# Expert weights for gate and up read in rows of 16 KB instead of 4 KB, in a one-core trunk step

## The chip, the core and the metric

The kernel runs on one core of a Trainium2 chip. The metric is the device time of one execution in microseconds (us): the median of three executions was 2595.72 us, the lowest 2595.25, the highest 2600.82.

## What is computed

One layer of a diffusion trunk with hybrid mixers, in fp32, for 512 latent tokens and 128 context tokens of 2048 channels: adaLN modulation, one input projection into attention heads and S5 groups, one output projection, and then a routed feed-forward network with 16 experts. Every expert picks its 64 best latent tokens and its 16 best context tokens. The change lies wholly in that last part:

```python
def expert_choice_ffn(x, p):
    B, L, D = x.shape
    cap = CAPACITY_FACTOR * L // N_EXPERTS
    aff = jax.nn.softmax((x @ p['w_router']).astype(jnp.float32), axis=-1)
    g, idx = lax.top_k(jnp.swapaxes(aff, 1, 2), cap)
    bidx = jnp.arange(B)[:, None, None]
    xs = x[bidx, idx]
    h = (jax.nn.silu(jnp.einsum('becd,edf->becf', xs, p['w_gate']))
         * jnp.einsum('becd,edf->becf', xs, p['w_up']))
    y = jnp.einsum('becf,efd->becd', h, p['w_down']) * g[..., None].astype(x.dtype)
    return jnp.zeros_like(x).at[bidx, idx].add(y)
```

w_gate and w_up are 16 x 2048 x 1024, w_down is 16 x 1024 x 2048, all fp32: 8 MB each per expert, 24 MB an expert, 384 MB in all. Every matrix is read once.

## The kernel before

It is written engine by engine, with semaphores set by hand. Up to about 1490 us it does the modulation, the projections, attention and S5, the output projection and the routing. Then the experts run one after the other on PE (TensorE), from fully unrolled code, while SP issues all weight transfers, POOL the gathers and scatters of tokens, and ACT and DVE evict and multiply.

**Pieces and the ring.** The weights of an expert come in 12 pieces of 2 MB. Pieces 0 to 7 are gate (even) and up (odd): piece j has 4 blocks of 128 channels, 4 * (j // 2) to 4 * (j // 2) + 3, each with all 1024 columns. Seen from a partition that is four rows of 1024 floats (4 KB), 512 KB apart in the matrix, since `w_gate_v` (L413) puts channel `k * 128 + p` into block k and partition p. Pieces 8 to 11 are down: two blocks of 128 hidden units each, rows of 2048 floats (8 KB). `piece` (L578) issues one piece into one of eight slots of the ring `w_ring` (L262). Two of the slots were in use earlier by other buffers, so that the first eight pieces (gate and up of expert 0) are issued one by one as space comes free.

**The order.** `ORDER` (L417) interleaves gate and up of expert e with down of expert e - 1, as PE uses them: two gate/up pieces, one down piece. `next_piece` (L606) waits until PE has used up the piece that lay in the slot eight pieces earlier (`s_used`), and then issues the next one; SP does nothing else in this stage.

**PE.** `expert` (L1438) goes through nine steps j. In step j it does `gate_up(j)` for expert e (for j < 8), `down(j - 1)` for expert e - 1 (for j > 0), and after steps 2, 4, 6 and 8 it turns four blocks of the tokens of expert e + 1 (`turn_four`, L1396). `gate_up` (L1410) waits for its piece, then uses each 64 columns of it as the stationary operand and the 80 turned tokens as the moving one, accumulating over all 2048 channels in PSUM. Each fp32 product shows as two MATMUL records and two LDWEIGHTS records, so that a piece makes 128 of each at L1419. `down` (L1424) has the tokens stationary and 512 columns moving (L1433). The first gate_up of an expert has to wait for ACT and DVE to take the hidden activations of the expert before out of PSUM (`s_hh`).

**Tokens.** `gather` on POOL (L1961) fetches the 80 rows of 8 KB of the expert's tokens into `xs`, one token to a partition. `turn_four` turns 80 x 128 columns at a time into PSUM bank 7 (through the helper at L985, where all turnings of the kernel have their records), and ACT (L962) copies four of them at a time to `xsT`, whose block k is the moving operand for block k of gate and up. `scatter` (L1971) adds the results to the rows of the output.

Of the kernel before, what the change touches and what calls it, by code (L numbers as in the profile page):

```python
# [13 lines left out]
P = 128  # L14
# [19 lines left out]
SLOTS = CAP_L + CAP_C  # L34
# [11 lines left out]
BIAS_OFF = [16, 8, 0]  # L46
START = 12
RING_SLOTS = 8


class Chain:
# [28 lines left out]
def trunk_step(nc, t, out):  # L80

    ctx = ExitStack()
    with ctx:
# [27 lines left out]
        def bank(b, n=BANK, at=0):  # L111
            return PS[:, b * BANK + at:b * BANK + at + n]
# [148 lines left out]
        RING = RING_SLOTS  # L261
        w_ring = [work[:, i * 4096:(i + 1) * 4096] for i in range(1, RING - 1)] + [hT_[:, 6144:6144 + 4096], work[:, 0:4096]]  # L262
        gate2 = mixT_[0:SLOTS, 0:D]
        xs = [mixT_[0:SLOTS, D * (1 + i):D * (2 + i)] for i in range(2)]
# [125 lines left out]
        s_w = [sem(f"s_w{i}") for i in range(RING)]  # L390
# [19 lines left out]
        w_in_v = t["w_in"].rearrange("(k p) n -> p k n", p=P)  # L410
        w_ada_v = t["w_ada"].rearrange("(k p) n -> p k n", p=P)
        w_out_v = t["w_out"].rearrange("(k p) n -> p k n", p=P)
        w_gate_v = t["w_gate"].rearrange("e (k p) n -> p e k n", p=P)  # L413
        w_up_v = t["w_up"].rearrange("e (k p) n -> p e k n", p=P)
        w_down_v = t["w_down"].rearrange("e (k p) n -> p e k n", p=P)

        ORDER = [0, 1, 8, 2, 3, 9, 4, 5, 10, 6, 7, 11]  # L417
# [28 lines left out]
        def _(sp):  # L446
# [5 lines left out]
            with sp.Fori(0, ADA_MIX // 2) as i:  # L452
                for s in range(2):
                    n = 2 * i + s
# [64 lines left out]
            for qc in range(16):  # L519
                src = bass.AP(t["rpb"].tensor, qc, [[RPB_W, 8], [RPB_W * RPB_H, HEADS], [1, SPAN]])  # L520
# [33 lines left out]
            for n in range(4):  # L554
                s = n % 2
# [22 lines left out]
            def piece(e, j, r):  # L578

                dst = w_ring[r % RING]  # L580
                if j < 8:
                    src = (w_gate_v, w_up_v)[j % 2][:, bass.ds(e, 1), 4 * (j // 2):4 * (j // 2) + 4, :]
                    dst = dst.rearrange("p (k n) -> p k n", k=4)
                else:
                    src = w_down_v[:, bass.ds(e, 1), 2 * (j - 8):2 * (j - 8) + 2, :]
                    dst = dst.rearrange("p (k n) -> p k n", k=2)
                sp.dma_start(dst, src.rearrange("p e k n -> p (e k) n")).then_inc(s_w[r % RING], 16)  # L587

            sp.wait_ge(s_omm, START + 15)
            piece(0, 0, 0)  # L590
# [26 lines left out]
            last = 24 * (EXPERTS // 2 - 1)  # L617
# [365 lines left out]
        def _(pe):  # L983
            def turn(dst, src, parts=P):
                return pe.transpose(dst, src, ident[0:parts, 0:parts])  # L985
# [398 lines left out]
            for tt in range(4):  # L1384
                pe.wait_ge(s_aff, tt + 1)
                last = turn(bank(0, P, P * tt)[0:EXPERTS, :], aff[:, tt, :])
# [9 lines left out]
            def turn_four(e, s, b):  # L1396

                pe.wait_ge(s_xsev, 4 * e + b)
                for k in range(4 * b, 4 * b + 4):
                    last = turn(bank(7, SLOTS, (k - 4 * b) * SLOTS), xs[s][:, k * P:(k + 1) * P], SLOTS)  # L1400
                last.then_inc(s_xsT, 1)

            def hidden_at(u, f):
# [644 lines left out]
```

## Time and profile before

| | |
|---|---|
| median of three runs | 2595.72 us |
| the profiled execution, its own time | 2594.34 us |
| its span, from the first instruction to the last | 2592.6 us |
| PE busy / PEld (weight loads, beside PE) | 2328.6 us (90%) / 1542.8 us (60%) |
| DVE, ACT, POOL busy | 583.8, 341.4, 291.2 us |
| bytes moved by DMA | 628.81 MB in 243174 packets |
| gate and up products (L1419), the slots in `work`, 14336 MATMUL | 540.6 us, 237 ns each |
| down products (L1433), 2688 MATMUL with tokens from `hT_` and weights from `work` | 310.8 us, 595 ns each |
| chain that ended last: SP's piece issues (L587) | 18% |

Matmuls overlap, so a mean of 237 ns is the length of one record and not its cost: the 128 records of one gate_up take 4.65 us together. PEld is the loading of the stationary operand, which runs beside PE. The granted clock (PEclk) is a share of full speed: 1.00 is 2.4 GHz, 0.50 is 1.2 GHz. "issue" is idle time of an engine in which it waited for nothing that the profile shows. A packet is one contiguous piece of a transfer that one of the 16 DMA engines moves; the share of a queue is the time that its packets took, of the time of all 16 engines in the window, and can come to a little over 100% because packets overlap.

### The profile page before, as it was taken

To read this page: it belongs to the slowest core of one execution; us is meant where nothing else is said; L and a number is where in the kernel's file an instruction comes from. 1 tells how busy PE (TensorE), PEld (TensorE's weight loads), DVE (VectorE), ACT (ScalarE), POOL (GpSimd) and SP (SyncE) were. 2 spreads that over 40 slices of the span, in tenths; PEclk is the share of its full clock that TensorE was granted. 3 is DMA by queue.
4 is the path that set the end of the run, shared out by engine and by line. 5 is a ranking of instruction groups with operands and counts; after the bars stand their busy time and mean duration, and the time that the engine had idled before them with its cause. 6 is when DMAs were issued, how large, how long until landed. Compare 5 with 4: busy or idle time off the path is not lost.

```text
span 2592.6 us, 57318 instructions
## 1 busy us (share of the span) xinstructions
PE 2328.6 (90%) x26381; PEld 1542.8 (60%) x26381; DVE 583.8 (23%) x882; ACT 341.4 (13%) x726; POOL 291.2 (11%) x375
## 2 busy tenths in 40 slices
PE   2599999999999999999999469999999998889997
PEld 1177888745555565554445366666666666666663
DVE  2242332034444433331103500000000000000001
ACT  2121111112322232321003100000000000000000
POOL 3060665000000000000021100000000000000000
PEclk8799999999999999999999689999999999999999
DMA  8921221585565621324222599999999999999996
GB/s 284 361 71 54 78 59 54 97 294 195 174 222 184 217 67 36 111 92 146 77 112 102 201 357 358 390 395 395 395 389 393 382 392 383 389 385 390 401 398 221
DMA packets 243174, 628.81 MB, mean 243 GB/s; under 512 B 14106, under 2 KB 96020, under 8 KB 220724
## 3 DMA queue, kind: packets, MB, share of 16 engines
q1 hardware_dynamic: 219904, 578.29, 59.6%
q0 software_dynamic: 3072, 20.97, 3.5%
q10 hardware_dynamic: 19972, 26.02, 3.1%
q8 instruction: 205, 3.36, 0.5%
q14 instruction: 21, 0.17, 0.0%
HBM read 600.77 MB, written 24.48 MB: 241 GB/s over the span
## 4 chain that ended last, share of the span: by engine, by line
PE 62%; SPq 18%; DMA 5%; DVE 4%; issue 3%; ACT 2%; ACTq 1%; POOL 0%; DVEq 0%; POOLq 0%
SPq L587 18%; PE PS L1239 14%; PE PS L1419 11%; PE PS L1330 11%; PE PS L1057 10%; PE PS L1433 6%; PE PS L985 2%; DMA work<-in_w_gate 2%; DVE work L1691 2%; PE PS L1267 2%; DMA work<-in_w_up 1%; PE PS L1227 1%; PE PS L1370 1%; PE PS L1252 1%; PE PS L1094 1%
## 5 line engine op out<-in xcount | busy, mean ns | idle before, releaser
L1419 PE MATMUL PS<-hT_,work 128*64 128x80 f32 x14336 | 540.6, 237 | 69.8 <-issue 54.9
L1419 PEld LDWEIGHTS PS<-hT_,work 128*64 128x64 f32 x14336 | 521.2, 140 | 115.0 <-issue 86.5
L1239 PE MATMUL PS<-hT_,work 128*128 128x512 f32 (+1 forms) x1536 | 439.4, 436 | 0.0
L1239 PEld LDWEIGHTS PS<-hT_,work 128*128 128x128 f32 x1536 | 223.8, 191 | 156.8 <-issue 156.8
L1433 PE MATMUL PS<-work,hT_ 128*32 128x512 f32 (+1 forms) x2688 | 310.8, 595 | 4.2 <-DVE mixT_ L1821 2.7
L1057 PE MATMUL PS<-work,hT_ 128*128 128x256 f32 x1280 | 284.5, 383 | 1.2 <-DVE hT_ L1555 1.2
L1330 PE MATMUL PS<-work,mixT_ 128*128 128x512 f32 x640 | 279.6, 597 | 0.0
L1057 PEld LDWEIGHTS PS<-work,hT_ 128*128 128x128 f32 x1280 | 243.5, 192 | 35.2 <-issue 2.1
L1807 DVE TENSOR_TENSOR hT_<-PS,hT_ 128x480 f32<-128x480 f32 x16 | 10.5, 657 | 982.3 <-ACT hT_ L968 982.3
L1330 PEld LDWEIGHTS PS<-work,mixT_ 128*128 128x128 f32 x640 | 121.7, 192 | 149.0 <-issue 149.0
L1433 PEld LDWEIGHTS PS<-work,hT_ 128*32 128x32 f32 (+1 forms) x2688 | 76.1, 105 | 163.8 <-issue 151.1
L962 ACT ACTIVATE hT_<-PS 128x320 f32<-128x320 f32 x64 | 28.0, 437 | 924.9 <-PE PS L985 924.9
L1691 DVE RECIPROCAL work<-work 128x640 f32<-128x640 f32 x24 | 99.7, 4153 | 158.9 <-ACT work L880 158.9
L1981 POOL DMA_INDIRECT out_y<-mixT_,work x16 | 23.0, 1440 | 861.6 <-DVE mixT_ L1821 861.6
L985 PE MATMUL PS<-consts,work 128*128 128x128 f32 (+3 forms) x441 | 68.2, 280 | 42.8 <-DVE work L1758 15.5
L985 PEld LDWEIGHTS PS<-consts,mixT_ 80*128 80x128 f32 (+3 forms) x403 | 39.8, 154 | 106.3 <-issue 65.5
L985 PE MATMUL PS<-consts,mixT_ 80*128 80x80 f32 (+3 forms) x403 | 52.1, 270 | 53.1 <-DVE mixT_ L1529 26.7
L1940 POOL TENSOR_TENSOR work<-work,consts 128x256 f32<-128x256 f32 x36 | 26.3, 760 | 623.6 <-DVE small L1677 548.0
L985 PEld LDWEIGHTS PS<-consts,work 128*128 128x128 f32 (+3 forms) x441 | 52.3, 151 | 52.0 <-DVE work L1758 16.0
L1009 PE MATMUL PS<-work,cT 128*2 128x512 f32 x256 | 40.2, 789 | 47.6 <-DMA work<-in_b_ada 47.6
L1419 PEld LDWEIGHTS PS<-hT_ 128*64 128x64 f32 x2048 | 72.0, 137 | 13.2 <-DMA hT_<-in_w_gate 8.6
L1419 PE MATMUL PS<-hT_ 128*64 128x80 f32 x2048 | 74.8, 233 | 5.4 <-DMA hT_<-in_w_gate 4.1
(241 smaller groups left out, 1656.4 us busy)
## 6 DMA issues: line engine op xcount, KB each, us to landing
work<-in_w_up SPq DMA_DIRECT2D x57, 2048.0 KB, 26.4
work<-in_w_down SPq DMA_DIRECT2D x56, 2048.0 KB, 26.7
work<-in_w_gate SPq DMA_DIRECT2D x55, 2048.0 KB, 23.9
work<-in_w_ada SPq DMA_DIRECT2D x32, 2048.0 KB, 9.4
work<-in_w_in SPq DMA_DIRECT2D x80, 512.0 KB, 4.8
work<-in_w_ada SPq DMA_DIRECT2D x8, 4096.0 KB
hT_<-in_w_gate SPq DMA_DIRECT2D x9, 2048.0 KB, 30.5
work<-in_w_out SPq DMA_DIRECT2D x4, 4096.0 KB, 13.7
```

Of the source, the lines that this page charges most:

```text
L587: sp.dma_start(dst, src.rearrange("p e k n -> p (e k) n")).then_inc(s_w[r % RING], 16)
L962: act.activation(xsT[s][:, 4 * b:4 * b + 4, :].rearrange("p k s -> p (k s)"), bank(7, 4 * SLOTS), ACT.Copy).then_inc(s_xsev, 1)
L985: return pe.transpose(dst, src, ident[0:parts, 0:parts])
L1009: last = pe.matmul(bank(2 + s)[q:q + 2, :], cTv[:, :, k], w_ada_ring[s][:, k, :], start=(k < 4), stop=(k >= KT - 4))
L1057: last = pe.matmul(bank(n % 2, 256), hT[:, k, tt * P:(tt + 1) * P], w_chunk[chunk % NW][:, 256 * (k % 4):256 * (k % 4) + 256], start=(k == ...
L1239: last = pe.matmul(bank(2 * which, n, col), w_chunk[chunk % NW][:, HD * (k % 8):HD * (k % 8) + HD], hT[:, k, col:col + n], start=(k == 0), ...
L1267: last = pe.matmul(bank(4)[q:q + 2, :], cTv[:, :, 8 * x + k], late_ring[x][:, k, :], start=(x == 0 and k < 4), stop=(x == 1 and k >= 4))
L1330: last = pe.matmul(bank(tt), mix_at(k)[:, tt * P:(tt + 1) * P], w_out_ring[n % 2][:, k, :], start=(k == 0), stop=(k == HEADS - 1 if n == 0 ...
L1419: last = pe.matmul(hidden_at(u, f)[64 * h:64 * h + 64, :], w[:, k % 4, f * P + 64 * h:f * P + 64 * h + 64], xsT[s][:, k, :], start=opens, ...
L1433: last = pe.matmul(bank(3 + c)[32 * g:32 * g + n, :], actT[s][:, k, first:first + n], w[:, k % 2, col * BANK:(col + 1) * BANK], start=(k = ...
L1691: ch.link(dve.reciprocal(rstd, rstd))
L1940: last = TT_(biasm[h % 2][:, v, :].rearrange("p (k i) -> p k i", i=8), view, masks[:, v, :].unsqueeze(2).to_broadcast([P, 32, 8]), ALU.add)
```

## The change

Another view of the channels: `(b p i)` in place of `(k p)`. Channel `512 * b + 4 * p + i` now lies in partition p as row i of block b, so that a partition's four rows of a piece are neighbours in the matrix: one row of 4 x 1024 floats, 16 KB, and a piece is 128 such rows, 2 MB without a gap. Its four blocks hold every fourth channel each instead of 128 neighbours. The sum over channels is the same if the tokens are turned to match, so `turn_four` takes every fourth column out of 512 (a step of 16 bytes) where it took 128 neighbours. Down's pieces, the ring, the order of the pieces, all waits, and the number and order of instructions on every engine stay as they are; SP's issues have the shape 128x4096 in place of 128x4x1024.

```diff
+NEAR = 4
...
-        w_gate_v = t["w_gate"].rearrange("e (k p) n -> p e k n", p=P)
-        w_up_v = t["w_up"].rearrange("e (k p) n -> p e k n", p=P)
+        w_gate_v = t["w_gate"].rearrange("e (b p i) n -> p e b i n", p=P, i=NEAR)
+        w_up_v = t["w_up"].rearrange("e (b p i) n -> p e b i n", p=P, i=NEAR)
...
                 dst = w_ring[r % RING]
                 if j < 8:
-                    src = (w_gate_v, w_up_v)[j % 2][:, bass.ds(e, 1), 4 * (j // 2):4 * (j // 2) + 4, :]
-                    dst = dst.rearrange("p (k n) -> p k n", k=4)
+                    n = 4 // NEAR
+                    src = (w_gate_v, w_up_v)[j % 2][:, bass.ds(e, 1), n * (j // 2):n * (j // 2) + n]
+                    src = src.rearrange("p e b i n -> p (e b) (i n)")
+                    dst = dst.rearrange("p (b n) -> p b n", b=n)
                 else:
                     src = w_down_v[:, bass.ds(e, 1), 2 * (j - 8):2 * (j - 8) + 2, :]
-                    dst = dst.rearrange("p (k n) -> p k n", k=2)
-                sp.dma_start(dst, src.rearrange("p e k n -> p (e k) n")).then_inc(s_w[r % RING], 16)
+                    src, dst = src.rearrange("p e k n -> p (e k) n"), dst.rearrange("p (k n) -> p k n", k=2)
+                sp.dma_start(dst, src).then_inc(s_w[r % RING], 16)
...
                 pe.wait_ge(s_xsev, 4 * e + b)
                 for k in range(4 * b, 4 * b + 4):
-                    last = turn(bank(7, SLOTS, (k - 4 * b) * SLOTS), xs[s][:, k * P:(k + 1) * P], SLOTS)
+                    rows = xs[s][:, k // NEAR * NEAR * P:(k // NEAR + 1) * NEAR * P].rearrange("t (p i) -> t i p", i=NEAR)
+                    last = turn(bank(7, SLOTS, (k - 4 * b) * SLOTS), rows[:, k % NEAR, :], SLOTS)
                 last.then_inc(s_xsT, 1)
```

## Rows read from the trace of the kernel before

**Rows 1.** Busy time by stretch: us, engines, PEclk, DMA share, GB/s; the expert stage
```profile
1620.71:2014.31 393.60, 367.96 (x7393) 259.83 (x7393) 31.78 (x49) 14.44 (x36) 16.55 (x24) 1.00 1.02 393
2014.31:2491.26 476.95, 434.71 (x8624) 309.85 (x8625) 37.05 (x57) 16.85 (x42) 18.14 (x26) 0.98 1.02 390
```
**Rows 2.** DMA queues, window 1620 to 2491: packets, MB, share of 16 engines
```profile
DMA packets 70632, 340.80 MB, mean 391 GB/s; under 512 B 2864, under 2 KB 2864, under 8 KB 55450
...
q1 hardware_dynamic: 68106, 322.36, 92.9%
q0 software_dynamic: 2400, 16.39, 8.0%
q8 instruction: 125, 2.05, 1.0%
```
**Rows 3.** PE's timeline, first gate_up of three experts: start us, us, instructions
```profile
1620.71 7.24 PE L1419 MATMUL PS<-hT_,work 128*64 128x80 f32 x203 [1.96 <-issue]
...
2014.31 9.71 PE L1419 MATMUL PS<-hT_,work 128*64 128x80 f32 x226 [1.96 <-issue]
...
2491.26 6.03 PE L1419 MATMUL PS<-hT_,work 128*64 128x80 f32 x168 [1.96 <-issue]
```
**Rows 4.** All waits of PE from 1600 to 2030: us, times, longest
```profile
PE PS L1419 <- issue: 24.0, 21, 2.0
PE PS L1433 <- issue: 2.4, 2, 1.6
PE PS L985 <- issue: 1.3, 1, 1.3
```
**Rows 5.** Waits of PE from 2030 to the end, those for weights
```profile
PE PS L1419 <- DMA work<-in_w_gate: 10.9, 8, 2.8
PE PS L1419 <- DMA hT_<-in_w_gate: 4.1, 3, 1.8
PE PS L1419 <- DMA work<-in_w_up: 2.7, 2, 1.5
...
PE PS L1433 <- DMA work<-in_w_down: 1.5, 3, 1.0
```
**Rows 6.** PE's timeline, three gate_ups that waited for their piece
```profile
2184.66 6.29 PE L1419 MATMUL PS<-hT_,work 128*64 128x80 f32 x128 [2.15 <-DMA work<-in_w_gate]
...
2520.06 4.65 PE L1419 MATMUL PS<-hT_ 128*64 128x80 f32 x128 [1.21 <-DMA hT_<-in_w_gate]
...
2536.11 4.65 PE L1419 MATMUL PS<-hT_,work 128*64 128x80 f32 x128 [1.40 <-DMA work<-in_w_gate]
```
**Rows 7.** DMA queues, window 60 to 70: w_ada, rows of 2 KB
```profile
q1 hardware_dynamic: 1901, 3.86, 104.4%
```
**Rows 8.** DMA queues, window 1137 to 1147: x read again, rows of 8 KB
```profile
q1 hardware_dynamic: 507, 4.15, 100.2%
```
**Rows 9.** Busy time by stretch, turn_b and the first token turnings: PEclk
```profile
138.80:142.80 4.00, 3.89 (x33) 3.73 (x33) 0.00 (x0) 1.76 (x10) 2.11 (x8) 0.50 0.81 257
1499.00:1504.00 5.00, 2.39 (x12) 1.67 (x12) 0.00 (x0) 0.96 (x3) 0.00 (x0) 0.50 1.02 255
```
**Rows 10.** Weight loads of those two stretches: busy us, mean ns
```profile
L985 PEld LDWEIGHTS PS<-consts,mixT_ 64*128 64x128 f32 x33 | 3.7, 206 | 2.4 <-issue 2.4
...
L985 PEld LDWEIGHTS PS<-consts,mixT_ 80*128 80x128 f32 x12 | 1.7, 217 | 13.2 <-DMA mixT_<-h_rows,work 11.6 <-ACT hT_ L962 1.6
```
**Rows 11.** PE's timeline, the first turning of gathered tokens
```profile
1500.38 0.80 PE L985 MATMUL PS<-consts,mixT_ 80*128 80x80 f32 x4 [11.46 <-DMA mixT_<-h_rows,work]
```
**Rows 12.** PE's timeline, gate_ups of expert 0, with no down between
```profile
1519.46 4.65 PE L1419 MATMUL PS<-hT_,work 128*64 128x80 f32 x128 [0.88 <-issue]
1525.66 4.65 PE L1419 MATMUL PS<-hT_,work 128*64 128x80 f32 x128 [1.55 <-issue]
1531.87 4.65 PE L1419 MATMUL PS<-hT_,work 128*64 128x80 f32 x128 [1.56 <-issue]
```
**Rows 13.** DMA packets, window 1524 to 1530
```profile
DMA packets 432, 2.52 MB, mean 421 GB/s; under 512 B 16, under 2 KB 16, under 8 KB 234
```

## The prediction

> **What bounds the kernel now.** The page puts TensorE first (PE busy 90% of the span) and a fifth of the final chain on SP's issues of weight pieces (L587, 18%). The change touches only the experts, so I read that stage alone, between the first turning of PE onto an expert at its steady pace and the last one. In its first 394 us and in its last 477 us PE is busy for 368 and 435 us, and the DMA engines stand at a share of 1.02 in both [rows 1]. Over 871 us the packets of the weight queue took 92.9% of the time of 16 engines, the gathers and scatters 8.0%, the instruction queue 1.0% [rows 2]: together 101.9%, so the DMA engines had no gaps. They moved 391 GB/s. An expert's first gate_up is easy to find in PE's timeline, since it always stands behind the same gap of 1.96 us (the wait for the hidden activations); those of experts 2, 8 and 15 start at 1620.71, 2014.31 and 2491.26 [rows 3]. The first six experts between them take 393.60 / 6 = 65.60 us each, the next seven 476.95 / 7 = 68.14 us, the mean of the thirteen is 66.97 us.
>
> Why are the first six faster if the DMA engines are full in both? Because PE takes its own pace while full slots lie ahead of it. Up to 2030 PE never waits for a weight piece, only for "issue", which is its own instruction stream [rows 4]. After 2030 it waits for gate, up and down pieces: 10.9 + 4.1 + 2.7 + 1.5 = 19.2 us in 17 waits [rows 5]. So two limits lie close together: PE's own pace, 65.6 us an expert, and the supply of weights, 67.0 us an expert. The supply is the slower by 1.37 us an expert, and the lead that the ring of eight slots gave, 6 x 1.37 = 8.2 us, is used up after six experts. A wait for weights also costs clock: the gate_up behind a gap of 2.15 us took 6.29 us where the others take 4.65 [rows 6].
>
> **The change, part by part.**
>
> *The rows of gate and up.* A piece is 2 MB as before, now 128 rows of 16 KB in place of 512 of 4 KB. The kernel has steady stretches of other row sizes. While only w_ada arrives (2 KB rows) 1901 packets took 104.4% of 16 engines for 10 us [rows 7], so one took 1.044 x 160 / 1901 = 87.9 ns. While x is read again (8 KB rows) 507 packets took 100.2% [rows 8]: 316 ns each. A line through the two has 37.2 ns per KB and 11.8 ns fixed per packet. It gives 164 ns for 4 KB and 620 ns for 16 KB; four rows of 4 KB are 656 ns, so each 16 KB saves about 35 ns. In the expert stage itself 4 KB rows were a little dearer. Of the packets of rows 2, 55450 - 2864 = 52586 are 4 KB rows; taking about 13100 of 8 KB at 316 ns out of 0.929 x 16 x 871 = 12946 us leaves 167 ns for one of them, and with that the saving is 50 ns. An expert has eight such pieces, 8 x 128 / 16 = 64 rows of 16 KB per DMA engine: 64 x 35 ns = **2.3 us less an expert** (3.2 by the second price; nothing if a packet has no fixed cost). The supply falls from 67.0 to about 64.7 us, below PE's 65.6. I take 2.3, because its two rows are of one size each.
>
> The sum hardly depends on it. PE's lead of 8.2 us, spread over the 14 experts that follow, lets the supply be 0.6 us slower than PE without a wait, so 66.2 us, a saving of 0.8 us, is nearly enough, and more than 1.4 us buys nothing, for PE's own pace takes over.
>
> The Trainium skill (DMA: Bandwidth & Descriptors, Why small descriptors are slow) speaks against this: it gives about 3 cycles of fixed cost per packet on the engine's internal bus, and calls joining descriptors worth it only at 256 B or less. By that advice the sum would be zero; taken at the 850 MHz that the page gives for the fabric, 3 cycles are 3.5 ns, an estimate of 0.7 us an expert. The trace disagrees with the size: 11.8 ns.
>
> *What becomes of it on PE.* The seven experts after 2014 go from 68.14 to 65.60 us: 7 x 2.54 = 17.8 us. The last expert, after 2491.26, has two waits of its own, 1.21 and 1.40 us [rows 6]: 2.6 us. The first experts gain nothing. From the other side: 19.2 us of waits and two slowed gate_ups of 1.6 us make 22.4 us, against 20.4 here; I take 20.4, since gaps partly take the place of "issue" gaps.
>
> *The token turnings.* The 16 turnings of an expert read every fourth column of a token, a step of 16 bytes, instead of 128 neighbours. Same number, same order. The step may cost weight-load time. The trace has a case: turn_b (L1026) loads every sixteenth column, a step of 64 bytes, at a granted clock of 0.50, and its 33 loads took 206 ns each; neighbours loaded at the same 0.50 at 1499 took 217 ns [rows 9, 10]. So a step costs nothing there, and I take zero. A step that doubled the load would cost at most 16 x 0.22 = 3.5 us an expert on PE; no row bears that out.
>
> *SP.* As many issues in the same order, with a quarter of the descriptors. SP's long issues come from full queues behind busy engines; shorter ones feed nothing faster. Zero.
>
> *The first gather.* PE is idle for 11.46 us before its first turning at 1500.38, waiting for this gather [rows 11], and weight pieces arrive at the same time. Each engine fetches 80 / 16 = 5 token rows; if each now stands behind one 16 KB packet instead of a 4 KB one, that is 5 x (620 - 164) = 2.3 us, at least 0. I take 1.1. Later gathers have most of an expert's time and are hidden; without that cover each would cost the same 2.3 us.
>
> **Sum**: -17.8 - 2.6 + 1.1 = -19.3 us. The profiled execution took 2594.34 us, so 2575.0; the median of the runs shown stands 1.4 us above it, which makes **2576 us**.
>
> **Rivals.**
>
> *A. The row size doesn't set the pace.* The engines might cut a 16 KB row again, or the memory and not the packet might set 391 GB/s. Then the supply stays at 67.0 us and the time at 2596. For it: I saw no weight row over 8 KB. Against it: 386 GB/s with 2 KB rows, 415 with 8 KB [rows 7, 8], and a queue that does carry 16 KB packets, the instruction queue [rows 2]. Chance 13%. A half-way case, a saving under 0.8 us an expert, gives about 2586; 7%.
>
> *B. Slower: the instruction stream waits behind long packets.* PE's instructions come by DMA in blocks of 16 KB: 125 packets for 13 experts [rows 2], 9.6 an expert. In stretches with nothing but gate_up, PE stops at each block: gate_ups of 4.65 us start 6.21 us apart [rows 12]. A block that stands behind one 16 KB weight packet arrives 0.46 us later. If PE feels that at every block, an expert takes 65.6 + 9.6 x 0.46 = 70.0 us; 15 x (70.0 - 67.0) = 45 us slower, about 2640. If it is felt only at the two or three blocks at an expert's start, 15 x 1.2 = 18 us eat the gain, and the time is about 2594. It decides once a block's arrival is later than PE's need of it. Against it: the distance is 6.20 us from 1519.46 on, when only gate and up pieces had been asked for until 1522, and 6.21 us from 1525.66 on [rows 12], when 432 - 234 = 198 of 432 packets were longer [rows 13]; it seems not to feel the packets beside it. The Trainium skill (Runtime: NRT & Kernel Launch, Instruction fetch mechanics) has blocks of 16 KiB fetched while the previous one runs, mostly hidden, with which the even 6.21 us agree. Chance 8%: 5% slower, 3% no difference.
>
> *C. Slower: a 16 KB row costs more than four of 4 KB.* The only 16 KB packets in the trace took 1.0% of 16 x 871 us / 125 = 1.1 us [rows 2], against the 656 ns at which this turns. At 1.1 us the supply would be 64 x 0.46 = 29 us an expert slower, near 3030 us. Those packets go elsewhere than SBUF and one at a time, so I give it 4%; a mild form (5% over the break-even, 2 us an expert) would give about 2626.
>
> That leaves 68% for the forecast, and with the half-way case 75% for faster.
>
> **The numbers.** 0.2% is 5 us, about what a measurement of this kernel can tell from no change. Faster by more: 0.75. Within: A and the mild B, 0.16. Slower: 0.09. The range goes from 2568 (the second price for packets, no gather cost, and some of PE's "issue" gaps gone with the traffic) to 2597, which takes in the half-way case and A; it leaves out the slower cases.
>
> **What would show it.** Right: the weight queue's packets in the expert stage fall to a third or so, none of gate and up under 8 KB; their share falls below 92%, and windows of the DMA share stand under 1.02; PE's waits for weights nearly vanish after 2030 while "issue" stays; experts come 65.6 us apart to the end; turnings of tokens take as long as before. Wrong: DMA share still 1.02 with the same GB/s (A), more "issue" idle and gate_ups over 6.21 us apart (B), fewer GB/s (C), or longer turnings.

## The result, and the profile after

| | before | the change |
|---|---|---|
| median of 16 executions each | 2597.49 us | 2603.76 us |
| lowest to highest | 2595.25 to 2601.46 us | 2593.92 to 2615.37 us |
| ratio of the change to before | | 1.0023, interval 1.0012 to 1.0033 |
| the profiled execution, its own time (span) | 2594.34 us (2592.6) | 2602.65 us (2600.9) |

The change is slower by 0.23%, some 6 us, where some 20 us less had been forecast (2576 us); the result lies outside the range that was given.

The page after names another limit. PE is busy for 23.6 us more, and the chain that ended last no longer has SP's piece issues in it, but PE's own products:

```profile
PE 2352.2 (90%) x26381; PEld 1561.9 (60%) x26381; DVE 584.4 (22%) x882; ACT 341.7 (13%) x726; POOL 291.5 (11%) x375
...
PE 83%; DVE 4%; issue 3%; ACT 2%; DMA 2%; ACTq 1%; SPq 0%; POOL 0%; DVEq 0%; POOLq 0%
```

The DMA queues over the same thirteen experts (window 1630.70 to 2501.71; packets, MB, share of 16 engines), which answer to [rows 2]:

```profile
DMA packets 31518, 344.51 MB, mean 396 GB/s; under 512 B 2889, under 2 KB 2889, under 8 KB 2889
...
q1 hardware_dynamic: 28992, 326.07, 91.7%
```

The rows of 4 KB are gone, the weight queue has 28992 packets where it had 68106, and the rate rose from 391 to 396 GB/s: the transfers became a little faster. All waits of PE in that window (us, times, longest), which answer to [rows 4, 5]:

```profile
PE PS L1423 <- issue: 51.6, 41, 2.1
PE PS L1437 <- issue: 4.0, 4, 2.2
PE PS L988 <- issue: 0.8, 1, 0.8
```

Not one wait for weights is left. The window of the same thirteen experts of before has 16.6 us of them, and 51.0 us of "issue" where 56.4 stand here. Yet the stage is no shorter. Busy time by stretch (us, then PE, PEld, DVE, ACT, POOL, PEclk, DMA share, GB/s), the first six of these experts and the next seven, which answer to [rows 1]:

```profile
1630.70:2033.99 403.29, 378.93 (x7392) 270.94 (x7393) 31.78 (x49) 14.45 (x36) 16.60 (x24) 0.98 1.01 395
2033.99:2501.71 467.72, 437.15 (x8625) 310.52 (x8625) 37.07 (x57) 16.85 (x42) 18.19 (x26) 0.99 1.01 396
```

The last seven did gain, from 68.14 to 467.72 / 7 = 66.82 us each. The first six lost more: from 65.60 to 403.29 / 6 = 67.21 us. That the loss lies in the first and the gain in the last has the clock in it: 1.00 and 0.98 before [rows 1], 0.98 and 0.99 here. Over the thirteen PE is busy for 816.08 us where it was 802.67. The largest piece of that stands in the token turnings (PE and PEld; busy us, mean ns, idle before):

```profile
L988 PE MATMUL PS<-consts,mixT_ 80*128 80x80 f32 x208 | 37.1, 300 | 0.8 <-issue 0.8
...
L988 PEld LDWEIGHTS PS<-consts,mixT_ 80*128 80x128 f32 x208 | 29.1, 213 | 45.2 <-issue 45.2
```

and before, same experts:

```profile
L985 PE MATMUL PS<-consts,mixT_ 80*128 80x80 f32 x208 | 26.0, 247 | 1.3 <-issue 1.3
...
L985 PEld LDWEIGHTS PS<-consts,mixT_ 80*128 80x128 f32 x208 | 17.7, 140 | 45.7 <-issue 45.7
```

The stepped weight load takes 213 ns where neighbours take 140. In the timeline four turnings show as 0.71 us where they were 0.50:

```profile
1764.81 10.65 PE L1423 MATMUL PS<-hT_,work 128*64 128x80 f32 x256 [1.96 <-issue]
...
1786.94 1.05 PE L1437 MATMUL PS<-hT_ 128*32 128x512 f32 x8 [2.18 <-issue]
1787.93 0.71 PE L988 MATMUL PS<-consts,mixT_ 80*128 80x80 f32 x4
```

**Where the 8.3 us between the two profiled spans lie** (after less before, by the same five marks in both timelines): +5.5 up to the issue of the first gather, +2.5 from there to the first gate_up, +1.9 in experts 0 and 1, +0.5 in the thirteen, -2.1 from expert 15 on. The first is not the change's doing: between the output projection's first product and the gather's issue the profile of before took 355.6 us, and every other profile of this case 358.0 to 360.9, also one of the kernel before in which nothing had been changed up to there (358.9). The granted clock goes with it. Busy times by stretch of before, then of the change, from the start to that product and from there to the gather:

```profile
0.00:1134.79 1134.79, 1018.63 (x5714) 677.36 (x5714) 403.37 (x588) 249.62 (x519) 212.64 (x302) 0.97 0.45 146
1134.79:1490.40 355.61, 321.30 (x958) 163.30 (x956) 95.57 (x166) 51.92 (x110) 34.57 (x10) 0.93 0.35 133
```

```profile
0.00:1136.94 1136.94, 1022.63 (x5713) 679.53 (x5714) 403.91 (x588) 249.89 (x519) 212.87 (x302) 0.96 0.45 146
1136.94:1495.90 358.96, 324.65 (x958) 164.78 (x956) 95.57 (x166) 51.93 (x110) 34.59 (x10) 0.92 0.35 132
```

The same products took PE 4.0 and 3.4 us longer at 0.96 and 0.92 than at 0.97 and 0.93. The profiled execution of before also lies below all 16 timed ones. What the change itself does is then about 3 us in these profiles and 6.3 by the medians (3.1 to 8.6 by the interval).

The terms of the thirteen experts are: -16.6 of waits for weights, +5.4 of "issue", +13.4 of busy PE. They add to +2.2 where the window grew by 0.5; records overlap a little at their ends, so the terms are good to some 2 us.

### The profile page after: what moved, and what is told of

The parts are those of the page before. It is cut to its first block, busy times and chain, and to the rows that moved or that the text cites. A ratio compares the mean times of both kernels' runs of the same rounds, so it can differ in the third digit from the quotient of the medians.

```text
span 2600.9 us, 57318 instructions
## 1 busy us (share of the span) xinstructions
PE 2352.2 (90%) x26381; PEld 1561.9 (60%) x26381; DVE 584.4 (22%) x882; ACT 341.7 (13%) x726; POOL 291.5 (11%) x375
## 4 chain that ended last, share of the span: by engine, by line
PE 83%; DVE 4%; issue 3%; ACT 2%; DMA 2%; ACTq 1%; SPq 0%; POOL 0%; DVEq 0%; POOLq 0%
PE PS L1423 24%; PE PS L1242 14%; PE PS L1437 13%; PE PS L1333 11%; PE PS L1060 10%; PE PS L988 3%; DVE work L1695 2%; PE PS L1270 2%; PE PS L1230 1%; PE PS L1373 1%; PE PS L1255 1%; PE PS L1097 1%; PE PS L1153 1%; ACTq L777 1%; PE PS L1201 1%
## 5 line engine op out<-in xcount | busy, mean ns | idle before, releaser
L1811 DVE TENSOR_TENSOR hT_<-PS,hT_ 128x480 f32<-128x480 f32 x16 | 10.5, 658 | 985.0 <-ACT hT_ L971 985.0
L988 PEld LDWEIGHTS PS<-consts,mixT_ 80*128 80x128 f32 (+3 forms) x403 | 52.1, 196 | 106.7 <-issue 65.2
L988 PE MATMUL PS<-consts,mixT_ 80*128 80x80 f32 (+3 forms) x403 | 64.0, 298 | 53.5 <-DVE mixT_ L1533 24.6
L1944 POOL TENSOR_TENSOR work<-work,consts 128x256 f32<-128x256 f32 x36 | 26.3, 760 | 626.4 <-DVE small L1681 553.5
```

Source lines behind the costliest of these rows:

```text
L1944: last = TT_(biasm[h % 2][:, v, :].rearrange("p (k i) -> p k i", i=8), view, masks[:, v, :].unsqueeze(2).to_broadcast([P, 32, 8]), ALU.add)
```

## The experiments

Twelve kernels. "Beyond fixed" is PE's "issue" idle over thirteen experts less 13 x 1.96 = 25.5 us, the gap that stands before every expert in every profile. "At 0.50" is the number of stretches over the thirteen experts in which the granted clock stood at 0.50; the first gate_ups below show that one costs about 1.6 us. "Gather first" holds three weight pieces back at the start, and the light kernels leave out most of up; both are explained below. Each ratio is to the kernel before as measured beside that kernel (medians of 2597.49 to 2598.92 us). The four light kernels, turnings only and rows only don't compute the reference. Lines in an experiment's rows are of its own kernel, a few off those of the change.

| kernel | median | ratio to before | thirteen experts | per expert | PE busy | issue beyond fixed | waits for weights | at 0.50 | GB/s |
|---|---|---|---|---|---|---|---|---|---|
| before | 2597.49 | | 870.55 | 66.97 | 802.67 | 25.5 | 16.6 | 7 | 391 |
| the change | 2603.76 | 1.0023 | 871.01 | 67.00 | 816.08 | 30.9 | 0 | 7 | 396 |
| turnings only | 2602.5 | 1.0012 | 872.37 | 67.11 | 815.71 | 24.8 | 8.1 | 9 | 391 |
| rows only | 2593.09 | 0.9982 | 860.51 | 66.19 | 804.71 | 32.1 | 0 | 6 | 398 |
| 8 KB rows, step 8 bytes | 2594.2 | 0.9979 | 862.09 | 66.31 | 812.79 | 17.8 | 7.6 | 7 | 398 |
| 16 KB, tokens sorted | 2595.61 | 0.9995 | 861.58 | 66.28 | 809.29 | 28.1 | 0 | 9 | 397 |
| 8 KB, tokens sorted | 2592.29 | 0.9967 | 859.86 | 66.14 | 804.19 | 23.8 | 6.1 | 8 | 398 |
| the change, gather first | 2596.93 | 1.0001 | 869.40 | 66.88 | 818.51 | 24.8 | 0 | 9 | 396 |
| before, gather first | 2594.39 | 0.9982 | 869.60 | 66.89 | 802.88 | 24.5 | 16.0 | 7 | 391 |
| 8 KB, sorted, gather first | 2581.68 | 0.9933 | 860.35 | 66.18 | 799.96 | 26.3 | 10.1 | 5 | 398 |
| light, 4 KB | 2546.59 | 0.9793 | 825.37 | 63.49 | 794.35 | 7.1 | 0 | 6 | 289 |
| light, 16 KB | 2561.2 | 0.9841 | 832.45 | 64.03 | 796.96 | 11.5 | 0 | 7 | 286 |
| light, 4 KB, gather first | 2548.44 | 0.9799 | 825.75 | 63.52 | 796.66 | 5.3 | 0 | 8 | 289 |
| light, 16 KB, gather first | 2554.93 | 0.9836 | 829.20 | 63.78 | 793.83 | 9.7 | 0 | 5 | 287 |

The change and the change with the gather first have the same program and the same rows in these thirteen experts, and yet their gaps beyond the fixed one are 30.9 and 24.8 us. Differences of gaps up to some 6 us between two profiles can be scatter.

### The two halves of the change, each alone

`e1_turnings_only` keeps before's rows of 4 KB and steps the turnings; `e2_rows_only` has the rows of 16 KB and turns neighbours.

```diff
 # turnings only: before, with
-                    last = turn(bank(7, SLOTS, (k - 4 * b) * SLOTS), xs[s][:, k * P:(k + 1) * P], SLOTS)
+                    rows = xs[s][:, k // NEAR * NEAR * P:(k // NEAR + 1) * NEAR * P].rearrange("t (p i) -> t i p", i=NEAR)
+                    last = turn(bank(7, SLOTS, (k - 4 * b) * SLOTS), rows[:, k % NEAR, :], SLOTS)
 # rows only: the change, with the reverse of these lines
```

> Pieces as before (rows of 4 KB), tokens turned with the step of 16 bytes; gate and up then meet the wrong channels of the tokens, everything else is computed as before. Theory T (the step itself makes a weight load longer once the clock is full, 0.71 us per four turnings in place of 0.50, as the profile of the change shows): PE's own pace goes from 65.6 to 66.5 us an expert, still under the supply's 67.0, so most of 64 x 0.21 = 13.4 us hides behind the supply; 2 to 6 us slower than before, about 2601. Theory R (the 16 KB rows slow PE's instruction stream and the gathers, and the turnings are longer only because of them): turnings at 0.50 us, time as before, 2597.

> Rows of 16 KB as in the change, but 128 neighbouring columns turned as before; gate and up again meet the wrong channels, the rest is computed as before. T: no waits for weights, turnings 0.50 us per four, experts 65.6 to 66.2 us apart, first gather 2 us later: 2597 - 20 + 2 = 2580, that is 0.991 to 0.995 of before. R: experts 67 us apart though PE never waits for weights, about 2600.

Measured: turnings only 2602.5 us, ratio 1.0012 (1.0002 to 1.0022); rows only 2593.09 us, ratio 0.9982 (0.9969 to 0.9995). PE and PEld of the turnings over thirteen experts, in turnings only:

```profile
L986 PE MATMUL PS<-consts,mixT_ 80*128 80x80 f32 x208 | 36.9, 300 | 0.0
...
L986 PEld LDWEIGHTS PS<-consts,mixT_ 80*128 80x128 f32 x208 | 29.1, 213 | 44.3 <-issue 44.3
```

and PE's waits in the same window of the same kernel:

```profile
PE PS L1421 <- issue: 47.2, 36, 2.5
PE PS L1435 <- issue: 3.1, 3, 1.5
PE PS L1421 <- DMA hT_<-in_w_gate: 2.9, 2, 2.3
PE PS L1421 <- DMA work<-in_w_up: 2.6, 2, 1.3
PE PS L1421 <- DMA work<-in_w_gate: 2.0, 1, 2.0
PE PS L1435 <- DMA work<-in_w_down: 0.6, 2, 0.3
```

The step alone makes PE busy for 13.0 us more, 10.9 of it in the turnings themselves. With 4 KB rows the supply sets the pace of the later experts, so part is hidden: waits for weights fall from 16.6 to 8.1 us, and the median rises by 4.3 us only. With 16 KB rows nothing hides it: from rows only to the change the medians stand 10.7 us apart, the thirteen experts 10.5 (8.9 to the change with the gather first). So the step is what made the change a loss. It is not the whole error, since rows only was expected to give close to the full forecast and gave 5 us (8 to 1 by the interval). Its waits in the window 1629.21 to 2489.72:

```profile
PE PS L1422 <- issue: 52.8, 43, 2.1
PE PS L1436 <- issue: 4.8, 4, 2.6
```

and its busy times in that window:

```profile
1629.21:2489.72 860.51, 804.71 (x16019) 567.60 (x16020) 68.83 (x105) 31.29 (x78) 34.70 (x50) 0.99 1.01 398
```

The waits for weights are gone here too, 16.6 us. But the "issue" gaps stand 6.6 us above those of before and PE's busy time 2.0, and the experts took only 10.0 us less. With the tokens sorted, 9.0 us less: there the gaps stand 2.6 us above, and PE's busy time 6.6, with two more stretches at 0.50.

### Rows of 8 KB, and tokens laid out once

If the step costs by its size, a step of 8 bytes should be cheaper; if the gaps come from long packets, shorter ones should help. `e3_rows_8k` is the change with two neighbouring channels to a partition. `e4_tokens_sorted` keeps 16 KB rows but lets DVE and POOL write the normalised tokens in the order in which PE wants them, so that each turning reads neighbours again.

```diff
 # 8 KB rows: the change, with
-NEAR = 4
+NEAR = 2
 # tokens sorted: the change, turnings as before, channel 1024 * h + 8 * p + i, and in the second norm
-                    last = STT(h2[tt % 2][:, cols], x1[:, tt, cols], stat[:, tt, 1:2], scale2[:, c, cols], ALU.mult, ALU.mult)
+                    last = STT(h2[tt % 2][:, cols].rearrange("t (i p) -> t p i", i=SPREAD), x1[:, tt, cols].rearrange("t (p i) -> t p i", i=SPREAD), stat[:, tt, 1:2],
+                               scale2[:, c, cols].rearrange("t (p i) -> t p i", i=SPREAD), ALU.mult, ALU.mult)
...
```

> Two neighbouring channels to a partition: rows of 8 KB, turnings with a step of 8 bytes; computes the reference. T: turnings lie between 0.50 and 0.71 us per four if the cost grows with the step, or at 0.71 if any step costs the same; supply near 65.5 us an expert by 12 ns a packet (128 packets fewer per engine and expert), so few waits; 2585 to 2600. R: half-way between before and the change in gathers and issue gaps, about 2600.

> Rows of 16 KB and turnings of 128 neighbours together, and the reference computed: the step is taken where DVE and POOL write the normalised tokens (eight neighbouring channels go to eight blocks), and once for the router's weights. T: as the run with rows only, 2580, plus what DVE and POOL lose by the step in five token tiles, 0 to 8 us, so 2580 to 2588. R: about 2600 or more.

Measured: 8 KB rows 2594.2 us, ratio 0.9979 (0.9967 to 0.9991); tokens sorted 2595.61 us, ratio 0.9995 (0.9983 to 1.0008). In the first the weight loads of the turnings cost the same with 8 bytes as with 16:

```profile
L988 PEld LDWEIGHTS PS<-consts,mixT_ 80*128 80x128 f32 x208 | 28.9, 212 | 44.4 <-issue 44.3
```

so that of these two steps the longer costs no more. And yet it is 9.6 us below the change, with intervals that don't touch: the rate is 398 GB/s, as high as with 16 KB rows, while the "issue" gaps beyond the fixed one fall from 30.9 to 17.8 us and 7.6 us of waits for weights take part of their place. 16 KB rows brought no more than 8 KB rows. And the stepped turnings cost little beside them: against the kernel with 8 KB rows and neighbours (below) PE is busy for 8.6 us more, but the experts take only 2.2 us longer, since the gaps are 6.0 us shorter. With 16 KB rows the step was felt in full, 8.9 to 10.5 us. Why it is felt so much less with 8 KB rows stays open; 6.0 us of gaps can be scatter.

Sorting the tokens gives back the turnings (the experts take 861.58 us) and pays elsewhere. DVE in the window 1150 to 1490 (busy us, mean ns), tokens sorted:

```profile
L1757 DVE TENSOR_TENSOR work<-work 128x1024 f32<-128x1024 f32 x5 | 21.7, 4343 | 0.2
L1750 DVE SCALAR_TENSOR_TENSOR work<-hT_,work 128x1024 f32<-128x1024 f32 x10 | 19.1, 1990 | 0.2
```

and before:

```profile
L1750 DVE TENSOR_TENSOR work<-work 128x1024 f32<-128x1024 f32 x5 | 16.3, 3251 | 0.2
...
L1745 DVE SCALAR_TENSOR_TENSOR work<-hT_,work 128x1024 f32<-128x1024 f32 x10 | 12.4, 1282 | 0.2
```

These add 12 us of DVE's time, mostly beside the output projection. The median is 8 us above the 2580 to 2588 us that had been expected. From its first product to the gather the profile took 358.0 us, no longer than others, so where the 2.5 us by which the median stands above rows only come from isn't shown, and the two intervals overlap.

### Is PE's pace its own?

The forecast took 65.6 us an expert as PE's own, whatever the DMA engines do. `e5_light_4k` (built on before) and `e6_light_16k` (built on rows only) leave out most of the transfers of up, so that a third of the traffic is gone; PE's program is unchanged.

```diff
 # light, 4 KB rows: before, with
+                    if j % 2 and not isinstance(e, int):
+                        src, dst = src[:, :, 0:1, 0:64], dst[:, 0:1, 0:64]
 # light, 16 KB rows: rows only, with
+                    if j % 2 and not isinstance(e, int):
+                        src, dst = src[:, :, 0:64], dst[:, :, 0:64]
```

> The kernel before, but from expert 1 on each piece of up brings only its first 64 columns of one row (256 B a partition in place of 16 KB); the rest of the slot keeps old weights, so the experts' products are not the reference's. A third of the weight traffic is gone and PE has the same instructions. Theory P (PE's own pace is set by its instructions, whatever moves beside it): no waits for weights, experts 66.2 us apart (the 860.5 us for thirteen of the run with rows only), issue idle about 57 us over them. Theory Q (the traffic slows the instruction blocks): 64 us or less apart and issue idle well under 45 us. Time 2588 by P, 2565 by Q.

> The same lightening (up pieces of 64 columns from expert 1 on) with gate in rows of 16 KB and neighbours turned; the experts' products are not the reference's. P: the same pace as the light kernel with 4 KB rows, within 0.3 us an expert. Q in the form that long packets hold the blocks up: 0.5 us or more an expert slower than that kernel, and more issue idle.

Measured: 2546.59 us, ratio 0.9793 (0.9779 to 0.9807), and 2561.2 us, ratio 0.9841 (0.9821 to 0.986). PE's waits over thirteen experts in the light kernel with 4 KB rows:

```profile
PE PS L1421 <- issue: 31.9, 21, 2.0
PE PS L987 <- issue: 0.7, 1, 0.7
```

and its busy times in the same window:

```profile
1632.58:2457.95 825.37, 794.35 (x16022) 565.43 (x16020) 68.80 (x105) 31.30 (x78) 34.69 (x50) 0.99 0.81 289
```

The pace is 63.49 us an expert, as theory Q had it (64 or less), and 2.1 us under what had been called PE's own; the time is below both forecasts. Of 25.5 us of gaps beyond the fixed one 7.1 are left, and PE's busy time fell from 802.67 to 794.35 us. At an expert's start, two gate_ups without a stop, in the light kernel, for two experts:

```profile
1632.36 9.07 PE L1421 MATMUL PS<-hT_,work 128*64 128x80 f32 x256 [1.96 <-issue]
...
1758.80 10.71 PE L1421 MATMUL PS<-hT_,work 128*64 128x80 f32 x256 [1.96 <-issue]
```

The second takes as long as the row at 1764.81 of the change (10.65 us). Both have the clock at 0.50 for a part. Busy times by stretch, the light kernel, then the change:

```profile
1632.36:1641.37 9.01, 9.01 (x257) 8.92 (x257) 4.30 (x6) 0.00 (x0) 2.62 (x3) 1.00 0.47 154
1760.20:1763.40 3.20, 3.20 (x53) 3.20 (x51) 2.97 (x4) 0.00 (x0) 0.00 (x0) 0.50 0.02 6
```

```profile
1764.80:1768.00 3.20, 3.19 (x48) 3.20 (x50) 3.07 (x5) 0.00 (x0) 0.00 (x0) 0.50 1.05 448
```

So a pair of gate_ups that takes 1.6 us longer is a matter of the clock and not of the traffic: the light kernels have 5 to 8 such stretches over thirteen experts and the others 5 to 9, each of them within 2 us of the end of a gap of 1.9 us or more. What the traffic makes is the gaps. In rows only the two gate_ups break off:

```profile
1629.11 7.31 PE L1422 MATMUL PS<-hT_,work 128*64 128x80 f32 x203 [1.96 <-issue]
1636.94 2.03 PE L1422 MATMUL PS<-hT_,work 128*64 128x80 f32 x53 [0.53 <-issue]
```

In such a gap PE waits for no semaphore that the trace shows, and all of its weights are there. It waits for its next block of instructions. They come by DMA, over the same engines: 125 packets of 16 KB over thirteen experts in each profile, one about every 7 us, and the packed trace has the time of each. Eight profiles have no waits for weights: the change, rows only, 16 KB with tokens sorted, the change with the gather first, and the four light kernels. They have 30, 30, 26, 26, 6, 8, 5 and 9 gaps over 0.3 us beside the fixed ones, and each of these 140 ends 1.2 to 1.7 us after an instruction packet has landed; gaps with another cause would end anywhere between two packets. The gaps also stand at the same places of the program: the one after the 9671st MATMUL record of the execution and the one after the 15680th are in all 14 profiles. No row of the profile names the packet as what ended a gap; it is the times that show it. The Trainium skill (Runtime: NRT & Kernel Launch, Instruction fetch mechanics) calls the fetch mostly hidden. By number that holds in both: 6 of 125 blocks left a gap in the light kernel, 30 in the change. By time it is 7.1 us beyond the fixed gaps there and 25.5 in before, beside full DMA engines: some 18 us more.

The light kernel with 16 KB rows took 832.45 us over its thirteen experts, 7.1 more, and 14.6 more in the median. I repeated the pair with the first gather out of the way (below), as `e11_light_4k_gather_first` and `e12_light_16k_gather_first`:

> The light kernel with 4 KB rows (up pieces of 64 columns from expert 1 on, so the experts' products are not the reference's) with the holding back. Without a gather beside weights and without waits for them, only the instruction blocks tell the row sizes apart. About 4 us under the light kernel, 2543; experts 63.5 us apart, issue idle beyond the fixed 25.5 us about 7 us.

> The same with 16 KB rows and neighbours turned. If long packets hold the instruction blocks up, it stays 5 to 10 us slower than the light kernel with 4 KB rows and the same holding back (0.4 to 0.7 us an expert, more issue idle); if the 14.6 us between the two light kernels came from the gather and from chance, under 3 us.

Measured: 2548.44 us, ratio 0.9799 (0.9775 to 0.9822), and 2554.93 us, ratio 0.9836 (0.9819 to 0.9853). PE's waits with 4 KB rows, then with 16 KB rows:

```profile
PE PS L1422 <- issue: 30.8, 21, 2.0
```

```profile
PE PS L1425 <- issue: 34.8, 21, 2.7
PE PS L1439 <- issue: 0.4, 1, 0.4
```

The experts again took longer with long rows, 829.20 against 825.75 us, and the gaps were longer by 4.4 us in both pairs. The two intervals of the last pair overlap in the whole time. In full traffic the four profiles with 16 KB rows have 24.8 to 32.1 us of gaps beyond the fixed one, the three with 4 KB rows 24.5 to 25.5. So no comparison has the sign the other way by more than 1 us, and the size, 0.3 to 0.5 us an expert in the light kernels (3.5 and 7.1 us over 13), is not settled.

### The first gather

In these kernels pieces 5 to 7 of expert 0 are held back until the tokens of expert 0 have landed. `e8_gather_first` is the change with it, `e10_before_gather_first` before with it.

```diff
+            sp.wait_ge(s_gath[0], 16)
             piece(0, 5, 5)
```

> The changed kernel with the pieces 5, 6 and 7 of expert 0 held back until the first gather has landed. If the weight packets beside the gather cost it its 13.9 us of PE idle: the first turning comes 5 to 8 us sooner after the gather's issue (17.9 us before), expert 0 does not wait for a piece, and the time is 4 to 7 us under the changed kernel, about 2598. If the gather has a latency of its own: no difference.

> The kernel before with the same holding back. The first gather is 3 to 5 us sooner; but here the supply of weights is the limit, and three pieces asked for 10 us later are 10 us of supply lost: by the theory that the supply bounds the second half, the gain at the gather comes back as waits for weights, so within 3 us of before, 2596 to 2600. If PE's pace alone bounds it: 2593.

Measured: 2596.93 us, ratio 1.0001 (0.9989 to 1.0014), which is 6.8 us below the change (5.7 by the ratios, whose intervals just overlap); and 2594.39 us, ratio 0.9982 (0.9971 to 0.9994), 4.5 us below before as measured beside it (2598.92). PE's first turning of gathered tokens, the change, and then the change with the gather first; both answer to [rows 11]:

```profile
1508.38 0.81 PE L988 MATMUL PS<-consts,mixT_ 80*128 80x80 f32 x4 [13.94 <-DMA mixT_<-h_rows,work]
```

```profile
1502.14 0.81 PE L989 MATMUL PS<-consts,mixT_ 80*128 80x80 f32 x4 [7.48 <-DMA mixT_<-h_rows,work]
```

From 11.46 us before, the wait grew to 13.94 with the long rows; without weights beside it, it is 7.48. So 4 us of before's wait and 6.5 of the change's are other transfers. The other profiles agree: from the gather's issue to the first gate_up it is 14.5 to 15.3 us beside 4 KB rows (three profiles), 16.0 and 16.2 beside 8 KB, 16.9 to 18.2 beside 16 KB (four), and 11.2 to 11.7 with the gather first (five). The light kernels gained nothing in their whole time by it, though (ratios 0.9793 and 0.9799 with 4 KB rows, 0.9841 and 0.9836 with 16 KB, 4 and 5 executions each), where 4 us had been expected; why, isn't shown.

### The parts that gained, together

`e7_rows_8k_sorted` has rows of 8 KB and tokens sorted in pairs by DVE and POOL (each of their operations on half the elements, twice); `e9_8k_sorted_gather_first` adds the gather's wait.

```diff
 # 8 KB, tokens sorted: the change, with
-NEAR = 4
+NEAR = 2
...
+                    for i in range(NEAR):
+                        last = STT(apart_of(h2[tt % 2][:, cols], i), pairs(x1[:, tt, cols], i), stat[:, tt, 1:2],
+                                   pairs(scale2[:, c, cols], i), ALU.mult, ALU.mult)
...
-                    rows = xs[s][:, k // NEAR * NEAR * P:(k // NEAR + 1) * NEAR * P].rearrange("t (p i) -> t i p", i=NEAR)
-                    last = turn(bank(7, SLOTS, (k - 4 * b) * SLOTS), rows[:, k % NEAR, :], SLOTS)
+                    last = turn(bank(7, SLOTS, (k - 4 * b) * SLOTS), xs[s][:, k * P:(k + 1) * P], SLOTS)
```

> Rows of 8 KB, and the tokens written sorted by DVE and POOL so that 128 neighbours are turned; computes the reference. T: the 8 KB rows gave 2594 with stepped turnings; these cost about 9 us there and DVE and POOL lose 2 to 4 us by their steps, so 2588 to 2591, faster than both kernels. If the 8 KB supply (398 GB/s, some waits for weights were left) is the limit instead, 2593 to 2595.

> Rows of 8 KB, sorted tokens, and the pieces 5 to 7 of expert 0 held back until the first gather has landed; computes the reference. The 8 KB rows with sorted tokens gave 2592 and holding back took 6.9 us off the changed kernel: with shorter packets the gather loses less, so 3 to 6 us off, 2586 to 2589, the fastest version. If the gather's gain is lost again at the ring (expert 0 late on its pieces, more waits for weights): 2592.

Measured: 2592.29 us, ratio 0.9967 (0.9954 to 0.9979), and **2581.68 us, ratio 0.9933 (0.9917 to 0.9948)**, the fastest kernel here that computes the reference, 17 us below before as measured beside it and 22 below the change. The last one's waits over thirteen experts (two rows of 1.0 and 0.2 us left out):

```profile
PE PS L1432 <- issue: 47.6, 37, 2.0
PE PS L1432 <- DMA work<-in_w_gate: 5.1, 4, 2.2
PE PS L1432 <- DMA hT_<-in_w_gate: 3.3, 2, 2.7
PE PS L1446 <- issue: 3.2, 3, 1.3
PE PS L1432 <- DMA work<-in_w_up: 1.5, 1, 1.5
```

and its busy times in the same window:

```profile
1621.26:2481.61 860.35, 799.96 (x16022) 566.76 (x16020) 68.85 (x105) 31.29 (x78) 34.78 (x50) 0.99 1.01 398
```

PE waits for weights again here, so the supply is near its limit with large rows: 860.35 / 13 = 66.2 us an expert (66.1 in its sibling). That is all that larger rows gave in these thirteen experts: 0.8 us each.

The gather's wait brought 10.6 us here (8.8 by the ratios), where it brought 5.7 and 4.5 elsewhere. The granted clock goes with the rest: the six executions of this kernel had 0.962 to 0.966 (median 0.964), the seven of its sibling 0.958 to 0.962 (median 0.961), and before beside it a median of 0.960. Over 2590 us 0.003 is 8 us of full clock, the most that it can be worth. So a part of the 17 us may be clock; whether this kernel holds a higher clock by its program or by chance wasn't tried.

## Why the prediction was wrong

**Right: what bounds the later experts.** PE waited for weights there, packets had a fixed cost, and larger rows took these waits away (16.6 us to none). Rival A, that the row size doesn't set the pace, falls: 391 GB/s became 396 and 398.

**Over-sized: "2.3 us less an expert".** 67.0 us was PE's mean over the thirteen experts, the first six of which drew on the lead of the ring, and not the supply's own pace. By bytes the weight queue of before brought 322.2 MB in 870.55 us, 68.0 us for the 25.17 MB of an expert, close to what the seven experts that waited took (68.14). In the change it brought 326.1 MB in 871.01 us, 67.2 us; with rows only and with 8 KB rows 66.8 to 66.9 us. So larger rows saved about 1.1 us an expert, and 0.8 in the change. By packets: an 8 KB row and a 16 KB row together should have taken 316 + 620 = 936 ns. The queue's 0.917 x 16 x 871.01 = 12779 us over about 13250 of each are 964 ns. As the text said, the sum should hardly have depended on it, and the waits did vanish. (A reading to set right: [rows 5] shows 16 waits, not 17; nothing hangs on it.)

**Wrong: "Because PE takes its own pace".** 65.6 us an expert was the pace of PE beside full DMA engines, read from the first six. With a third of the traffic gone the same program takes 63.5. And it was not to be had for the last seven: with 16 KB rows, neighbours turned and no wait for weights, PE took 66.2 and 66.3 us an expert (rows only, tokens sorted); in rows only it was 65.7 for the first six and 66.6 for the last seven. The clock has a part in that: of the stretches at 0.50, one of the seven of before lies in its first six experts, and all six of rows only lie in its last seven, so that 65.6 us was a pace with hardly any of them. Of 16.6 us of waits that were removed 10.0 and 9.0 were saved; the rest came back as "issue" gaps (6.6 and 2.6 us more) and as busy time (2.0 and 6.6 more, with one stretch at 0.50 fewer and two more). The one allowance for it, from 22.4 to 20.4 us, "since gaps partly take the place of "issue" gaps", had the right sign and a third of the size. Instead of 17.8 us the rows gave 10.0 in the thirteen experts.

**Rival B was right in kind.** It was set aside because gate_ups in the first expert came 6.20 and 6.21 us apart with few and with many long packets beside them [rows 12]. That distance says nothing of the mixed stage: with a third less traffic 5 to 9 blocks of instructions are late for PE over thirteen experts, beside full DMA engines 26 to 30. Its price of up to 45 us was far too high: what the longer packets alone add to the gaps is 4.4 us over thirteen experts in the light kernels, and between nothing and 7 us in full traffic.

**Wrong: "a step costs nothing there, and I take zero".** This step decided the sign. The rows compared were both at a granted clock of 0.50 [rows 9, 10]. There it is true of the change too (busy times by stretch, its first turnings; PEclk is the 0.50):

```profile
1508.00:1513.50 5.50, 3.23 (x16) 2.26 (x16) 0.00 (x0) 1.53 (x4) 0.09 (x1) 0.50 1.01 287
```

and the weight loads in that stretch:

```profile
L988 PEld LDWEIGHTS PS<-consts,mixT_ 80*128 80x128 f32 x16 | 2.3, 216 | 16.4 <-DMA mixT_<-h_rows,work 14.1 <-ACT hT_ L965 2.4
```

A stepped load takes 216 ns at 0.50, and neighbours took 217. At the full clock neighbours fall to 140 ns and stepped ones stay at 213. Read from these four figures, the stepped load has a floor of its own that doesn't follow PE's clock, and at half clock it costs nothing beside the slower one. Nearly all turnings run at full clock. The cost is 52 groups of four x (0.71 - 0.50) = 10.9 us over thirteen experts and 60 x 0.21 = 12.6 in all, since the first expert's four groups ran at 0.50. The bound that was written down ("at most 3.5 us an expert") was wide enough, and the range left it out.

**Near: the first gather**, 1.1 us taken, 0 to 2.3 as bounds, 2.5 measured between the two profiles. SP's shorter issues at zero: nothing in the runs speaks against it (the chain's 18% on them went to 0% and the time did not fall).

**The sum again.** For the thirteen experts: rows -10.0, turnings +10.5, together +0.5. With the gather's +2.5, +1.9 in experts 0 and 1 (which have their share of stepped turnings, and no waits for weights to save) and -2.1 at the end, it is +2.8 in the profiles. The medians say +6.3. What lies between the two is not explained. That the change's executions scatter over 21 us is in part the clock: its three fastest, 2593.92 to 2596.73 us, had 0.962 to 0.965, and its two at 0.957 took 2607.66 and 2607.97; but its slowest, 2615.37, had 0.960. Before's 16 scatter over 6 us, and in the later measurements, with 17 to 35 executions, over 12 to 13.

## What to carry to other kernels

Price an operation at the clock at which it will run: two kinds that cost the same at 0.50 can differ by half at 1.00, and a comparison at the lower clock hides exactly the term that is sought. "PE never waits for data in this stretch" does not make its pace its own; look at the same program beside less traffic before counting on that pace, and expect a part of the waits for transfers that are removed to come back elsewhere (here 6.6 and 7.6 of 16.6 us). Before going to the longest row, try the one between: here 8 KB rows gave the same 398 GB/s as 16 KB rows, and the cheapest gain, a gather that goes ahead of three bulk transfers nobody needs yet (4.5 and 5.7 us), had nothing to do with row sizes. And before a difference of a few us is put down to a change, compare the granted clocks.

## What the runs showed of the hardware that was not expected

- A fp32 weight load of 80x128 whose columns are 8 or 16 bytes apart takes 212 or 213 ns at full clock, against 140 ns for neighbours, and 216 against 217 at half clock.
- Twice the row length helps, and twice again does not: 391 GB/s with 4 KB, 398 with 8 KB, 396 to 398 with 16 KB, all with down's 8 KB rows beside them.
- PE's "issue" idle depends on what the DMA engines carry: 51.0 us over thirteen experts at 391 GB/s, 32.6 and 30.8 us at 289 GB/s, with the same instructions. In the eight profiles without waits for weights all 140 such gaps over 0.3 us, beside the fixed ones, end 1.2 to 1.7 us after a 16 KB instruction packet has landed.
- Some 3.2 us at a granted clock of 0.50 made a pair of gate_ups 1.6 us longer, with a third less traffic and with full traffic alike (10.71 and 10.65 against 9.07 us). A profile has 5 to 9 such stretches over thirteen experts, whatever the row size.
- DVE and POOL pay for stepped fp32 operands (a step of 32 bytes): 1990 against 1282 ns and 4343 against 3251 ns for 128x1024 on DVE, 4186 against 3162 ns on POOL. One DVE operation that wasn't edited took 1107 ns a piece in place of 704 in the same profile:

```profile
L1737 DVE TENSOR_TENSOR hT_<-hT_,work 128x512 f32<-128x512 f32 x20 | 22.1, 1107 | 0.7
```

  It runs in the same stretch as POOL's stepped additions; whether these slow it was not tried.
